# Two-stack transformer forward pass on one core: input in two halves and bias lines later, clearing moved behind scalings, output rows transposed earlier

## The reference, cut to what matters

```python
x = layer_norm(x, ln0_g, ln0_b)                       # the first thing done
for l in range(2):                                    # first stack
    mix = hybrid_mixer(x, ...)     # pooling, differential attention, bidirectional recurrence
    x = layer_norm(alpha * x + mix, ln1_g[l], ln1_b[l])
    hid = square(relu(x @ w_up[l]))
    x = layer_norm(alpha * x + hid @ w_down[l], ln2_g[l], ln2_b[l])

h = concatenate([pad, meta_tokens, x], axis=1)        # second stack
for l in range(2):
    h = hybrid_layer(h, pos, ...)  # starts with rmsnorm(h); three attentions, gates, h + merged @ w_out
h = rmsnorm(h, final_g)
return h[:, 128:]                                     # 512 rows of 1024

def diff_attention(...):                              # in hybrid_mixer
    bias = rel_table[rel_bucket(k_pos[None] - q_pos[:, None])]   # depends on k_pos - q_pos alone
    logits = logits + bias
def rmsnorm(x, g):
    return x * rsqrt(mean(x * x, -1) + 1e-6) * g
```

## Time and profile before

| | |
|---|---|
| time, median of 3 runs | 3973.81 us (3973.63 to 3974.01) |
| the profiled execution's own time | 3973.54 us |
| its span | 3971.7 us |
| mean granted TensorE clock | 0.993 |
| TensorE busy | 3856.0 us, 97% of the span |
| VectorE busy | 2119.3 us, 53% |
| ScalarE busy | 945.3 us, 24% |
| GpSimd busy | 1188.9 us, 30% |

### The profile page before, as it was taken

The page is one execution under the profiler, slowest core; times in us unless marked ns, Lnnn a source line. Parts: engine busy times, 40 slices in busy tenths (PEclk is TensorE's granted clock), DMA queues, the critical chain, the costliest instruction groups (busy, mean ns, idle before and its releaser), DMA issues.

```text
span 3971.7 us, 69185 instructions
## 1 busy us (share of the span) xinstructions
PE 3856.0 (97%) x27480; PEld 3131.0 (79%) x27480; DVE 2119.3 (53%) x4847; ACT 945.3 (24%) x2399; POOL 1188.9 (30%) x962
## 2 busy tenths in 40 slices
PE   9999989999999999999999999899999999999999
PEld 5667678888888666678888888787887788888778
DVE  5666665576413666575566611533446662444566
ACT  4133321122101233222113200323322212333221
POOL 0113315434442023133543443102333130142322
PEclk9999999999999999999999999999999999999999
DMA  3111102222222110112222222211211231121222
GB/s 132 34 38 43 38 18 86 90 71 89 85 85 80 55 47 33 34 33 72 85 90 75 85 86 88 72 59 54 65 59 59 86 96 59 54 67 59 62 64 96
DMA packets 70959, 266.61 MB, mean 67 GB/s; under 512 B 7872, under 2 KB 8000, under 8 KB 69872
## 3 DMA queue, kind: packets, MB, share of 16 engines
q1 hardware_dynamic: 68160, 246.42, 19.7%
q10 hardware_dynamic: 2480, 15.76, 1.1%
HBM read 253.64 MB, written 8.52 MB: 66 GB/s over the span
## 4 chain that ended last, share of the span: by engine, by line
PE 91%; DVE 6%; DVEq 1%; issue 1%; ACT 1%; DMA 0%; PEld 0%; ACTq 0%; PEldq 0%; SPq 0%
PE ps L2675 33%; PE ps L1589 16%; PE ps L1615 10%; PE ps L2630 8%; PE ps L1634 2%; PE ps L1716 2%; PE ps L962 2%; PE ps L1776 2%; PE ps L918 2%; PE ps L2641 1%; PE ps L1735 1%; PE ps L2619 1%; PE ps L2689 1%; PE ps L952 1%; PE ps L2707 1%
## 5 line engine op out<-in xcount | busy, mean ns | idle before, releaser
L2675 PE MATMUL ps<-arena,ring 128*128 128x256 f32 x1856 | 430.3, 379 | 0.0
L2675 PEld LDWEIGHTS ps<-arena,ring 128*128 128x128 f32 x1856 | 352.7, 190 | 47.8
L2675 PE MATMUL ps<-arena 128*128 128x256 f32 x1536 | 360.9, 379 | 0.0
L2391 POOL TENSOR_TENSOR arena<-ring 128x512 f32<-128x512 f32 x50 | 63.7, 1274 | 967.9 <-DMA ring<-in_weights 732.4
L2533 POOL TENSOR_TENSOR arena<-ring 128x512 f32<-128x512 f32 (+1 forms) x120 | 144.5, 1204 | 688.6 <-DMA ring<-in_weights 573.6
L2630 PE MATMUL ps<-xT,ring 128*128 128x512 f32 x768 | 342.4, 600 | 0.6 <-DMA ring<-in_weights 0.6
L2675 PEld LDWEIGHTS ps<-arena 128*128 128x128 f32 x1536 | 291.9, 190 | 39.6
L2630 PEld LDWEIGHTS ps<-xT,ring 128*128 128x128 f32 x768 | 143.9, 191 | 179.8 <-issue 178.8
L1615 PE MATMUL ps<-arena,ring 128*128 128x264 f32 (+1 forms) x896 | 207.9, 388 | 15.3 <-DVE arena L2327 10.5
L2675 PE MATMUL ps<-xT,ring 128*128 128x256 f32 x896 | 203.7, 380 | 4.2 <-ACT xT L2853 2.3
L1615 PEld LDWEIGHTS ps<-arena,ring 128*128 128x128 f32 x896 | 169.2, 192 | 46.1 <-issue 13.2
(11 more groups left out here) (428 smaller groups left out, 7552.2 us busy)
## 6 DMA issues: line engine op xcount, KB each, us to landing
ring<-in_weights SPq DMA_DIRECT2D x459, 512.0 KB, 3.5
h_dram<-arena ACTq DMA_DIRECT2D x2, 2112.0 KB, 6.9
arena<-h_dram ACTq DMA_DIRECT2D x2, 2112.0 KB, 9.4
arena<-skew_dram ACTq DMA_DIRECT2D x8, 448.0 KB, 3.2
arena<-in_x SPq DMA_DIRECT2D x1, 2048.0 KB, 7.9
out_rows<-arena SPq DMA_DIRECT2D x8, 256.0 KB, 2.8
skew_dram<-arena ACTq DMA_DIRECT2D x4, 511.5 KB, 7.0
consts<-in_const SPq DMA_DIRECT2D x1, 1256.0 KB, 10.4
```

Of the source, the lines that this page charges most:

```text
L2675: m = pe.matmul(bank_of(i, n), w[name][:, k, :], x[name](k), start=start and k == ks[0], stop=stop and k == ks[-1], skip_group_check=True)
```

## The change

Setup: the first constants and `x` are issued first, `x` in two transfers by columns (512 of 1024 each), with a semaphore each; tiles `x0` to `x3` wait only for the first. No lines are made at the start. Both groups of lines are made among the first projections: heads 0 and 1 behind `lows`, heads 2 and 3 behind `zk`. Seam: the scalings into `xg` come ahead of the clearing. End: ScalarE copies half 0 of the rows from PSUM, unscaled, while the last pair's products run; so the same four banks serve half 1, whose blocks 4 and 5 are transposed behind product 7, 6 and 7 at the end; the sum of squares goes to TensorE in three pieces instead of two; ScalarE scales its half in place in SBUF and issues its own four stores.

```diff
@@ SP @@
+            sp.dma_start(c1[:, 0:early], const1[:, 0:early]).then_inc(first_loaded, 16)
+            for h in range(2):
+                sp.dma_start(xrow[:, :, 512 * h:512 * h + 512], x_in.rearrange("(t p) d -> p t d", p=P)[:, :, 512 * h:512 * h + 512])\
+                  .then_inc(x_loaded[h], 16)
             sp.dma_start(relb[0:32, :], rel_bias).then_inc(rel_loaded, 16)
             sp.dma_start(oh[0:32, 0:LINE], onehot).then_inc(rel_loaded, 16)
-            sp.dma_start(c1[:, 0:early], const1[:, 0:early]).then_inc(first_loaded, 16)
-            sp.dma_start(xrow, x_in.rearrange("(t p) d -> p t d", p=P)).then_inc(x_loaded, 16)
             sp.dma_start(c1[:, early:K1_N], const1[:, early:K1_N]).then_inc(c_loaded, 16)
...
             for t in range(4):
-                sp.wait_ge(*at("end_a", 0, t))
-                sp.dma_start(out[t * P:(t + 1) * P, 0:512], rows_out[:, t, 0:512]).then_inc(out_stored, 16)
                 sp.wait_ge(*at("end_d", 0, t))
                 sp.dma_start(out[t * P:(t + 1) * P, 512:1024], rows_out[:, t, 512:1024]).then_inc(out_stored, 16)
@@ TensorE, setup @@
-            pe.wait_ge(*at("relw", 0))
-            for h in range(2):
-                for i in range(2):
-                    n = min(512, LINE - 512 * i)
-                    o = a.open(f"line{h}_{i}")
-                    a.close(pe.matmul(o[:, 0:n], relw[0:32, h, :], oh[0:32, 512 * i:512 * i + n], start=True, stop=True))
             pe.wait_ge(first_loaded, 16)
-            pe.wait_ge(x_loaded, 16)
             for j in range(KD):
+                pe.wait_ge(x_loaded[j // 4], 16)
                 turn(a, f"x{j}", [xrow[:, t, j * P:(j + 1) * P] for t in range(4)])
...
-                for n in ("zk", "zr"):
-                    proj(a, f"{n}@0", ws[0], xT)
+                if L == 0:
+                    pe.wait_ge(*at("relw", 0))
+                    bias_lines(0)
+                proj(a, "zk@0", ws[0], xT)
+                if L == 0:
+                    pe.wait_ge(*at("line_taken", 0))
+                    bias_lines(1)
+                proj(a, "zr@0", ws[0], xT)
@@ VectorE, seam @@
+            for j in range(KD):
+                dve.wait_ge(*at("h0_ready", 0, j))
+                ts(xg[:, j, :], hT[:, j, :], gain(0, j), None, ALU.mult).then_inc(STEPS["xg"][0], 1)
             for z in (sel, ptm, vc[:, 0, :], vb[:, 0, :], negc, v2[:, :, 0, :]):
                 dve.memset(z, 0.0)
...
             dve.wait_ge(c2_loaded, 32)
-            for j in range(KD):
-                dve.wait_ge(*at("h0_ready", 0, j))
-                ts(xg[:, j, :], hT[:, j, :], gain(0, j), None, ALU.mult).then_inc(STEPS["xg"][0], 1)
@@ TensorE, end: row_square(src, place) opens the sum at place 0 and closes it at place 2 @@
+            def turn_rows(i, js):
+                for j in js:
+                    pe.wait_ge(*at("xg", LAYERS, j))
+                for t in range(4):
+                    if i:
+                        pe.wait_ge(*at("end_copied", 0, t))
+                    for j in js:
+                        mm = pe.transpose(ps[:, END_BANK[t], j % 4 * P:j % 4 * P + P], xg[:, j, META + t * P:META + (t + 1) * P], i2)
+                    if js[-1] % 4 == 3:
+                        mm.then_inc(STEPS["end_made"][0], 1)
...
+                    if L == LAYERS - 1 and u[1] == ("out", 6):
+                        if hf == 3:
+                            turn_rows(1, range(4, 6))
+                        if hf == 5:
+                            pe.wait_ge(*at("squares_summed", L))
+                            row_square(sqsum, 0)
+                        if hf == 6:
+                            pe.wait_ge(*at("sq2", LAYERS, 6))
+                            row_square(sq2[:, 6, :], 1)
+                            turn_rows(1, [6])
+                            pe.wait_ge(*at("sq2", LAYERS, 7))
+                            row_square(sq2[:, 7, :], 2)
+                            turn_rows(1, [7])
@@ ScalarE, end @@
+                elif kind == "pair" and u[1] == ("out", 6) and hf == 2 and L == LAYERS - 1:
+                    for t in range(4):
+                        act.wait_ge(*at("end_made", 0, t))
+                        act.activation(rows_out[:, t, 0:512], ps[:, END_BANK[t], :], ACT.Copy).then_inc(STEPS["end_copied"][0], 1)
...
             for t in range(4):
-                act.wait_ge(*at("end_made", 0, t))
-                act.activation(rows_out[:, t, 0:512], ps[:, END_BANK[t, 0], :], ACT.Copy, scale=ec[:, 8 + t:9 + t])\
-                   .then_inc(STEPS["end_a"][0], 1)
+                act.activation(rows_out[:, t, 0:512], rows_out[:, t, 0:512], ACT.Copy, scale=ec[:, 8 + t:9 + t])
+                act.drain()
+                act.dma_start(out[t * P:(t + 1) * P, 0:512], rows_out[:, t, 0:512]).then_inc(out_stored, 16)
@@ VectorE, end: in add_out; next_norm no longer adds squares for blocks 6 and 7 of the last layer @@
                 if name == "6":
                     stt(p2, o, 0.5, p1, ALU.mult, ALU.add).then_inc(taken_, 1)
+                    if L == LAYERS - 1 and j == KD - 2:
+                        dve.wait_ge(*at("sq2", LAYERS, 5))
+                        tt(sqsum, sqsum, sq2[:, 5, :], ALU.add)
+                        did("squares_summed")
```

More of the change, by code:

```diff
@@ L479, in build @@
         c_loaded = sem("c_loaded")
-        x_loaded = sem("x_loaded")
+        x_loaded = [sem(f"x_loaded{i}") for i in range(2)]
         first_loaded, rel_loaded = sem("first_loaded"), sem("rel_loaded")
@@ L611, in build @@
         step("end_made", 8)
-        step("end_a", 4)
+        step("end_copied", 4)
         step("end_d", 4)
@@ L683, in build @@
         BA, BV = [0, 1, 2], [3, 4, 5, 6, 7]
-        lines = [[f"line{h}_{i}" for h in (2 * k, 2 * k + 1) for i in range(2)] for k in range(2)]
-        setupA = Tiles(lines[0] + [f"x{j}" for j in range(KD)], BA)
+        setupA = Tiles([f"x{j}" for j in range(KD)], BA)
         LN_FIRST, LN_UP, LN_NEXT = (3, 4, 5, 6), (0, 1, 2, 3), (0, 1, 3, 4)
@@ L1793, in mean_square_rest, with row_square @@
                 mm.then_inc(STEPS["ms_made"][0], 1)
-            def row_square(src, first_):
+            def row_square(src, place):
                 for t in range(4):
                     mm = pe.matmul(ps[:, SB, t:t + 1], src[:, META + t * P:META + (t + 1) * P], ones[:, 0:1],
-                                   start=first_ and t == 0, stop=not first_ and t == 3, skip_group_check=True)
-                if not first_:
+                                   start=place == 0 and t == 0, stop=place == 2 and t == 3, skip_group_check=True)
+                if place == 2:
                     mm.then_inc(STEPS["rows_made"][0], 1)
-            def turn_rows(t, i):
-                if i and END_BANK[t, i] in FB:
-                    pe.wait_ge(*taken(max(k for k in range(len(HALVES)) if FB[k % 3] == END_BANK[t, i])))
-                if (t, i) == (3, 1):
-                    pe.wait_ge(*at("end_a", 0, 0))
-                for j in range(4):
-                    pe.wait_ge(*at("xg", LAYERS, 4 * i + j))
-                    mm = pe.transpose(ps[:, END_BANK[t, i], j * P:(j + 1) * P], xg[:, 4 * i + j, META + t * P:META + (t + 1) * P], i2)
-                mm.then_inc(STEPS["end_made"][0], 1)
+            def turn_rows(i, js):
[8 more added lines that the diff above has]
+                        mm.then_inc(STEPS["end_made"][0], 1)
             pe.wait_ge(c2_loaded, 32)
@@ L1836, in stack2_pe @@
                     if L == LAYERS - 1 and u[1] == ("out", 4) and hf == 6:
-                        for t in range(4):
-                            turn_rows(t, 0)
+                        turn_rows(0, range(4))
+                    if L == LAYERS - 1 and u[1] == ("out", 6):
[11 more added lines that the diff above has]
+                            turn_rows(1, [7])
                 if L < LAYERS - 1:
@@ L2199, in add_out @@
                     next_norm(L, j + 1)
-                    if j + 1 == KD - 1:
+                    if j + 1 == KD - 1 and L < LAYERS - 1:
                         did("squares_summed")
@@ L2206, in next_norm @@
                 ts(xg[:, j, :], hT[:, j, :], gain(L + 1, j), None, ALU.mult).then_inc(STEPS["xg"][0], 1)
-                if j > 1:
+                if j > 1 and (j < 6 or L < LAYERS - 1):
                     dve.wait_ge(*at("sq2", L + 1, j - 1))
@@ L2805, in _, with bias_lines @@
             a = Taker(act, setupA, 0, a_made, a_taken)
[L2807 removed]
+            def bias_lines(k):
+                for b in range(4):
+                    h, i = 2 * k + b // 2, b % 2
+                    n = min(512, LINE - 512 * i)
+                    act.wait_ge(*at("line_made", k, b))
+                    m = act.activation(line[:, h, 512 * i:512 * i + n], ps[:, BV[1 + b], 0:n], ACT.Copy)
+                m.then_inc(STEPS["line_taken"][0], 1)
                 act.drain()
[L2810 removed]
+                for h in (2 * k, 2 * k + 1):
```

(10 more changed lines are left out.)

28 lines of the change are left out of this document (6 added, 22 removed).

## The result

The changed kernel takes 3981.69 us, the median of 14 runs (3976.41 to 3986.55); the kernel before took 3971.9 us on the same chips (14 runs, 3967.84 to 3977.11). The ratio is 1.0025, with a 95% interval of 1.0018 to 1.0033: a small loss, against a forecast of 3977.8 us and "no change that can be told". The forecast's range holds the time; the sum behind it does not describe what happened. A fifth term was missing, a wait of 7.6 us and the half speed that followed it, and one of the four, the line groups, was far too large; the two partly cancelled.

A forecast was written before the change was run, and what follows sets the result against it. TensorE's own work, 91% of the chain, was taken as the bound. Terms +0.9 + 6.8 - 3.4 - 0.3 = +4.0 on 3973.54 gave 3977.5, with 0.27 for the median 3977.8 us; range 3970.5 to 3982.0.

The forecast's parts named there:

- Setup, input first: Setup: the mean comes 0.6 us earlier, but TensorE idles and its clock falls; +0.9 us, bounds -1.4 and +2.6.
- the 4.0 read at the seam: Seam between the stacks: TensorE's clock is back at full speed 4.0 us after work restarts; applied to setup.
- the upper bound: Setup's worst case, +2.6 us: the clock returns about 3.5 us later than taken.
- Lines behind projections: First projections: a second line group costs 3.4 us of work and 3.4 lost at half speed; +6.8 us.
- My first rival: First projections: second line group leaves the clock alone, sum +0.6, 3974.4 us; both escaping, -2.8, 3971.0; chance 0.25.
- The slower rival: First projections: clock doesn't return between the line groups; +10.2 instead of +6.8, sum up to +9.1, 3982.9 us; chance 0.07.
- The rule I weighed: First projections: without idle gaps the clock stays up, so the second line group costs 3.4 us, not 6.8.
- Seam: Between the stacks: scalings start 3.42 us earlier, so TensorE idles less; -3.4 us, bounds -5.1 to -1.7.
- End: Output: first stores at 3964.2 instead of 3964.52, then DMA engines are full; -0.3 us, bounds -0.6 and +1.2.

The follow-up runs named there:

- The twins: Kernel before with twelve more line-group products, 32 rows in one, 128 in the other: 3993.17 and 3995.93 us with 32, 3986.12 and 3986.25 with 128.

## Why the prediction came out as it did

*Setup, input first (+0.9).* The mechanism held: the constants land at 13.03 (12.9 taken), the mean is at 18.62 (18.4), and the clock falls in the gap. The size was at the unfavourable side of its bounds, +2.0: full speed came back at about 24.5, not 22.4. With the padding closed early it was +0.6 at the projections. The return took 3.3 to 5.9 us of work in these profiles, so the 4.0 read at the seam was one value of several; the 3.5 us of delay behind the upper bound came from no row, and 2.1 was measured.

*What lies behind the variance: a missing term, +10.1.* The working went from the variance straight to the lines and took the low-rank projections to start as before. This is the step that failed. In the whole diff the line that makes the list, `setupA = Tiles(...)`, loses the four line names (the excerpt under The change leaves that line out), and the class `Tiles`, which pads such lists, stands right behind the first line that the diff changes; I checked what each removed instruction cost and not what the list's length set. The chain shown above is 7.6 of wait and 2.5 of half speed.

*Lines behind projections (+6.8).* Mis-sized: 3.4 for the work was right (3.63), but the fall of the clock, taken from one execution's windows as a fixed price, is an event that comes in some executions. Of eleven 32-row groups behind projections in the profiles taken (without those of sixteen products) five were followed by a low stretch, four of about 3.4 us and the one I took my price from of 6.8. Such stretches cost half their length, (4 x 1.7 + 3.4) / 11 = 0.9 a group on average, so by this estimate a group is worth 3.6 + 0.9 = 4.5. The term should have been about +4.5 between medians, and 2 x 4.5 - 7.0 = +2.0 against the profiled execution, which had its worst case; it read +0.5, since neither group met a fall. My first rival, both groups escaping, is what this stretch did. The slower rival (no return between the groups) did not happen in any profile.

*The rule I weighed.* The Trainium skill ("TensorE: Matmul & The Clock Gate", section "Why this matters for your kernels") has the clock kept up by having no idle gap. I set it aside because the fall in the earlier trace rows came without one. The twins bear that out, TensorE busy throughout and the clock down for 24 us; in the changed kernel the price that the prediction drew from this rule, 3.4 a group, was nonetheless near the 3.6 measured. Absence of gaps is not sufficient here; it was enough for six of eleven groups of four.

*Seam (-3.4).* Right: TensorE idle for 6.85 to 6.87 us in the seven kernels that have the edit, 10.50 or 10.51 in those that don't, and nothing handed back in the stretch behind it; over the whole second stack the spread between executions is too wide to tell.

*End (-0.3).* Right: -0.2 against the old end with the clock held longest (19.59 against 19.79); the pair of profiles read -0.8, since the execution of before lost its clock there earlier.

So the forecast of 3977.8 came near 3981.7 because +10.1 that was missing met 6.3 that was charged too much; the rest is +1.1 in setup and small differences behind it. That the range holds the time is luck in a second way. The forecast started from three runs with a median of 3973.81, and over fourteen runs the kernel before has 3971.9. As a change, +4.0 was forecast and +9.8 measured. That is more than the 7.9 us which the prediction gave a chance of 0.09 to be passed upward; added to 3973.81 it would have come to 3983.6, outside the range.

## What to carry to other kernels

When a change shortens or lengthens a list that hands out buffers in turns, look at what its length sets (padding, base counts, who gives back the last turn, and how late in that engine's program), not only at the instructions that come and go. Sixteen products on 32 of TensorE's rows lowered its clock for themselves and the work behind them, and groups of four did so in five cases of eleven. Clearing the unused rows in idle time of another engine and using all 128 costs TensorE no time (3.43 us a group instead of 3.62). Neither of the two groups changed in this way among the projections was followed by a low stretch; with two cases that can be chance, so it is worth trying and not yet shown. A price read from a single execution's clock needs a second execution before it stands in a sum as certain.

## What the runs showed of the hardware that I had not expected

- With sixteen products of 32 rows the granted clock was 0.50 for 24 us, TensorE busy in every window; with twelve of the sixteen over 128 rows (and other values) it stayed at 1.00. Two executions each.
- In the second execution with sixteen products of 32 rows the clock also fell at about 19.2 us, behind an idle time of only 1.83 us in setup, and cost 1.2 us up to the low-rank projections; in the other eight executions with that setup, idle times of 1.33 to 1.91 us left it at 1.00.
- The same code's granted clock differs between executions. The kernel before ran from 3966.64 to 3978.8 us over all its runs, 12 us, where its first three runs spanned 0.4; with eleven runs of a kernel the ratio's interval was still 0.0009 to either side.
- The output's stores filled the DMA engines whichever queue issued them (share 1.01 and 1.02 in the changed kernel's windows from 3974 to 3978, 1.00 before): from the first issue to the end of the span it is 7.18 us with SP alone and 7.3 with SP and ScalarE.
